# Two quads of saved block products in chunks 2 to 7 of gate and up, and Silu on ScalarE

## The chip, the cores and the metric

The kernel runs on one core of a Trainium2 chip. The metric is the device time of one execution in microseconds (us), the median of three runs. Inside the core, TensorE (PE) multiplies, ScalarE (ACT) and VectorE (DVE) work element by element, GpSimd (POOL) does little here, and SyncE (SP) issues the weight loads. Each engine takes its own instructions strictly in the order written, and waits at semaphores for the others.

## The reference, cut to what matters

The block is a feed-forward net (FFN), a token mixer, and a second FFN, on 256 tokens of width 2048, in float32. Both FFNs have 5632 hidden columns:

```python
def swiglu(x, w_gate, w_up, w_down):
    return (jax.nn.silu(x @ w_gate) * (x @ w_up)) @ w_down

h = layer_norm(ALPHA * h + 0.5 * swiglu(h, w_gate, w_up, w_down), g, b)   # twice, with the mixer between
```

The change concerns the two products `x @ w_gate` and `x @ w_up` of both FFNs and the silu and the product that follow.

## The kernel before, in words

**Units and splits.** The hidden columns are worked in 11 chunks of 512. For a chunk, the 2048 inner rows come as 8 units of 256 rows for the gate and 8 for the up weights. The loads (512 KB each) go to a ring of 8 raw slots, strictly in order; a raw slot is loaded again when VectorE is through with it (`lo_done`). Each float32 number is split in a high part, a copy on ScalarE in a reduced format (`chunk_hi`, L1142), and a low part, a subtraction on VectorE (`chunk_lo`, L1149). The pair lies in one of 4 split slots, which comes free when TensorE has used the item in it (`unit_used`). TensorE waits for the low part and then makes three products a tile, high by high, high by low, low by high (`token_mm`, L628 to L630). A unit is 2 token halves by 2 inner tiles by 3 products, 12 matmuls of 128x128 by 512 columns.

**Quads.** In chunks 2 to 10, one pair (a, b) of the inner units, 6 and 7, is treated together with the gate and the up columns as a 2 by 2 block matrix, for which two token halves would need 8 block products. Winograd's form of Strassen's scheme does it in 7, called P1 to P7, each on one 512-column item with 2 x 3 = 6 matmuls (`chunk_form`, L1266 to L1268). A quad thus takes 7 x 6 = 42 matmuls in place of the 48 of its four units. The price is on the other engines: seven splits in place of four, and four sums of weight blocks on VectorE (`chunk_add`, L1538; they feed the splits of P5, P6, P7 and P4), two seeds of the up accumulators (`up_seeds`, L1546 and L1549) and three ScalarE copies of half accumulators (L1382, L1393, L1398).

P1, P5, P6 and P7 of the next chunk's quad stand in the second half of a chunk, between the up units; P2, P3 and P4 in the first half, between the gate units. A loop chunk of before is this list of 19 items (g gate unit, u up unit):

```
g0 P2 g1 P3 g2 P4 g3 g4 g5 | u0 u1 P1 u2 P5 P6 u3 P7 u4 u5
```

**Order on the engines.** All orders are written out by hand. ScalarE and VectorE run 3 items ahead (`CHUNK_LEAD`), one split an item, the sums and the other work set between splits at fixed items. When the gate is done, ScalarE takes `tanh(0.5 g)` of both halves (`tanh_gate`, L1350), and VectorE makes `(tanh + 1) g` of it in two instructions (`gate_part`, L1490). At the start of a chunk VectorE multiplies the last chunk's gate by its up (`gate_times_up`, L1211, two instructions), then writes the seeds. After item 4 TensorE transposes the 4 x 2 tiles of the last chunk's result (`hT_pe`, L1192), split again by ScalarE and VectorE behind their item 8.

Chunk 0 (16 units) and chunk 1 are written out, chunks 2 to 9 are a hardware loop, chunk 10 is written out.

Of the kernel before, what the change touches and what calls it, by code (L numbers as in the profile page):

```python
# [12 lines left out]
ALU = mybir.AluOpType  # L13
# [6 lines left out]
P = 128  # L20
# [37 lines left out]
class Chunk:  # L58


    def __init__(self, items, raws, slots):
        self.items, self.raws, self.slots = items, raws, slots
# [5 lines left out]
    def raw(self, u, c, ahead):  # L68

        return self.raws.index((u, c, ahead)) if (u, c, ahead) in self.raws else None  # L70

    def used_before(self, i):

        n = len(self.items)
        back = [v for v in range(i) if self.slots[v] == self.slots[i]]
        return back[-1] if back else max(v for v in range(n) if self.slots[v] == self.slots[i]) - n


def chunk_plans(a, b, units):


    def plain(c, us):
        return [("unit", u, c) for u in us]

    some = [u for u in range(units) if u not in (a, b)]
    gate, up = plain(0, some), plain(1, some)
    here = [gate[0], ("P2", 0, 0), gate[1], ("P3", 0, 0), gate[2], ("P4", 0, 0), *gate[3:]]
    ahead = up[:2]
    ahead += [("P1", 0, 0), up[2], ("P5", 0, 0), ("P6", 0, 0), up[3], ("P7", 0, 0), *up[4:]]
    raws_here = [(some[0], 0, 0), (b, 0, 0)] + [(u, 0, 0) for u in some[1:]]  # L90
    u1 = [(u, 1, 0) for u in some]
    raws_ahead = u1[:2] + [(a, 0, 1), (a, 1, 1), u1[2], (b, 1, 1), *u1[3:]]
    lead = plain(0, range(units)) + plain(1, (a, b)) + ahead
    raws_lead = [(u, 0, 0) for u in range(units)] + [(a, 1, 0), (b, 1, 0)] + raws_ahead
    body, last = here + ahead, here + up
    shift = len(here) - 1
    return (Chunk(lead, raws_lead, [i % 4 for i in range(len(lead))]),
            Chunk(body, raws_here + raws_ahead, [(i + (i >= shift)) % 4 for i in range(len(body))]),
            Chunk(last, raws_here + u1, [i % SPLIT_SLOTS for i in range(len(last))]))
# [159 lines left out]
def hybrid_block(nc, x, x_t, ffn1_w_gate, ffn1_w_up, ffn1_w_down, ln1_g, ln1_b, w_in, q_norm_g, kv_norm_g,  # L259
# [40 lines left out]
    (F1GU, F1G1, F1GL, F1GE, F1DA, F1DB, WA, WZ, WB, WC, WQI, WUQ, WO,  # L300
     F2GU, F2G1, F2GL, F2GE, F2DA, F2DB) = range(19)
    QUAD_A, QUAD_B = KU - 2, KU - 1
    CHUNKS = chunk_plans(QUAD_A, QUAD_B, KU)
    LOOP_FROM, LOOP_TO = 2, GATE_CHUNKS - 1
    CHUNK_LEAD = 3

    def gate_up_phases(ffn):

        lead, body, last = CHUNKS
        n, m = len(lead.raws), len(body.raws)  # L310
        assert m % RAW_SLOTS == 0 and (2 * KU) % RAW_SLOTS == 0 and (n + len(last.raws)) % RAW_SLOTS == 0
# [36 lines left out]
    with ExitStack() as ctx:  # L348
# [168 lines left out]
        def split_place(p, it, u):  # L517

            n = st.phases[p].units
            if chunk_of(p) is not None:  # L520
                round, v = divmod(u, n)
                plan, s = chunk_of(p), chunk_of(p).slots[v]
                before = plan.used_before(v)
                if before < 0 and p in (F1G1, F2G1):
                    last = [w for w in range(2 * KU) if ring_place(w, 2 * KU, SPLIT_SLOTS) == s]
                    before = last[-1] - 2 * KU if last else None
                elif before < 0 and p in (F1GE, F2GE):
                    before = CHUNKS[1].used_before(CHUNKS[1].slots.index(s))
                free = None if before is None else st.index(p, it, round * n + before + 1)
                return (whi, wlo, s, free) if s < SPLIT_SLOTS else (chunk_hi4, chunk_lo4, 0, free)  # L530
# [3 lines left out]
            if plan_of(p) is not None:  # L534
                f, pair = (0, 1)[p in DOWN[1]], (0, 1)[p in (F1DB, F2DB)]
                s, before = SPLITS[pair][u] if u < n else (u - n, LAST_USER[u - n])
                if before is not None:
                    free = st.index(DOWN[f][before[0]], 0, before[1] + 1)
                elif s < SPLIT_SLOTS:
                    last = [v for v, slot in enumerate(CHUNKS[2].slots) if slot == s][-1]  # L540
                    free = st.index(GE[f], 0, last + 1)
                else:
                    free = None
# [409 lines left out]
        G1, GL, GE = [F1G1, F2G1], [F1GL, F2GL], [F1GE, F2GE]  # L953
        EXITS, ENTRIES = (F1DB, WO, F2DB), (WA, F2GU)
# [35 lines left out]
        def ffn_loads(sp, f, w_gate, w_up, w_down, load_x):  # L990
# [4 lines left out]
            def released(plan, r):  # L995

                u, c, ahead = plan.raws[r]
                if u == QUAD_B and c == 0 and not ahead and ("P4", 0, 0) in plan.items:
                    return plan.at("P4") - 1
                if (u, c, ahead) == (QUAD_A, 0, 1):  # L1000
                    return plan.at("P1") + 1
                if (u, c, ahead) == (QUAD_A, 1, 1):
                    return plan.at("P7")
                if (u, c, ahead) == (QUAD_B, 1, 1):
                    return len(plan.items) + CHUNKS[1].at("P3")
                return plan.at("unit", u, c)

            def raw_free(p, it, r):

                plan = chunk_of(p)  # L1010
                if r >= RAW_SLOTS:
                    return st.index(p, it, released(plan, r - RAW_SLOTS) + 1)
                if p == G1[f]:
                    return st.index(GU[f], 0, 2 * KU - RAW_SLOTS + r + 1)
                body = CHUNKS[1]
                return st.index(p, it, released(body, len(body.raws) - RAW_SLOTS + r) - len(body.items) + 1)

            lead, body = CHUNKS[:2]
            assert all(released(lead, len(lead.raws) - RAW_SLOTS + r) - len(lead.items)
                       == released(body, len(body.raws) - RAW_SLOTS + r) - len(body.items) for r in range(RAW_SLOTS))  # L1020
# [18 lines left out]
            gate_up(GE[f], 0, GATE_CHUNKS - 1)  # L1039
# [21 lines left out]
        DOWN_SCALE = 0.25 / ALPHA  # L1061
# [11 lines left out]
        BODY_STEPS = ["U4", "V", "P4", "P5", "P6", "P7"]  # L1073
        LOOPS = LOOP_TO - LOOP_FROM
        GU_STEPS = len(SUM_STEPS) + len(BODY_STEPS) * (LOOPS + 1) - 3 + 3
        F_STEPS = GU_STEPS + len(SUM_STEPS) + sum(PAIR_STEPS)
        BODY_ACTS = ["P1 out", "U2 out", "U3 out"]
        GU_ACTS = 4 + len(BODY_ACTS) * (LOOPS + 1)
        F_ACTS = GU_ACTS + 4 + len(PAIRS)

# [4 lines left out]
        def round_of(p, it):  # L1085

            return -1 if p in G1 else LOOPS if p in GE else it

        def in_chunk(f, p, it, step):

            first = F_STEPS * f + len(SUM_STEPS) + len(BODY_STEPS) - 3
            return round_of(p, it) * len(BODY_STEPS) + (first + BODY_STEPS.index(step) + 1)

        def before_chunk(f, p, it, step):

            first = F_STEPS * f + len(SUM_STEPS) - 3
# [2103 lines left out]
```

## Time and profile before

| | |
|---|---|
| median of three runs | 1897.35 us (1897.04 to 1897.39) |
| the profiled execution's own time | 1897.86 us |
| its span, first to last instruction | 1896.1 us |
| PE busy | 1878.8 us, 99% |
| DVE busy | 1428.4 us, 75% |
| ACT busy | 980.6 us, 52% |
| DMA | 189 GB/s mean |
| granted TensorE clock, mean | 0.998 |

The page's busy share of PE counts any matmul in flight, so 99% says that PE hardly ever stood empty. The share of the other engines is a mean over stretches in which they run against a full queue and stretches in which they wait.

### The profile page before, as it was taken

Reading aid. Unit: us, or ns where it says so; the run is one execution under the profiler, and the core shown is the slowest. Engines: PE = TensorE matmul, PEld = TensorE weight load, DVE = VectorE, ACT = ScalarE, POOL = GpSimd, SP = SyncE. Lnnn points to the kernel's source line nnn. Section 1 sums busy time; section 2 is a strip of 40 time slices with the busy share of each in tenths; the row PEclk is TensorE's granted clock in tenths of the full one; section 3 lists DMA queues with packets and bytes.
Section 4 is the critical chain, followed back from the end, with each engine's and each line's share of the span. In section 5 each row is a group of like instructions: output and inputs, shape, how many; then the busy total and the mean of one; then the engine's idle time right before and its main releaser. Section 6 shows DMA issues by size and latency. Waiting matters only on the chain.

```text
span 1896.1 us, 28377 instructions
## 1 busy us (share of the span) xinstructions
PE 1878.8 (99%) x10382; PEld 1602.2 (85%) x10382; DVE 1428.4 (75%) x1601; ACT 980.6 (52%) x1112; POOL 66.9 (4%) x93
## 2 busy tenths in 40 slices
PE   9999999999999999999999999999999999999997
PEld 8888888888888888999999888888888888888886
DVE  5777777777788896677766967677777777688887
ACT  5555555555455553545744534455555555455452
POOL 0000000000000001300131100000000000000000
PEclk9999999999999999999999999999999999999999
DMA  8555566656655584755442067546665555646654
GB/s 304 168 183 177 190 211 213 211 203 217 206 177 189 204 312 118 222 181 150 130 135 91 23 205 261 178 129 213 212 211 188 188 178 198 222 134 222 216 184 188
DMA packets 185375, 357.50 MB, mean 189 GB/s; under 512 B 11328, under 2 KB 23616, under 8 KB 184272
## 3 DMA queue, kind: packets, MB, share of 16 engines
q1 hardware_dynamic: 183600, 347.43, 54.6%
q0 software_dynamic: 1696, 8.99, 1.4%
q8 instruction: 53, 0.87, 0.2%
q14 instruction: 26, 0.21, 0.0%
HBM read 354.28 MB, written 2.10 MB: 188 GB/s over the span
## 4 chain that ended last, share of the span: by engine, by line
PE 95%; DVE 3%; issue 1%; ACT 1%; DMA 0%; POOLq 0%; POOL 0%; DVEq 0%; ACTq 0%
PE acc L628 22%; PE acc L630 21%; PE acc L629 21%; PE acc L652 3%; PE acc L656 3%; PE acc L654 3%; PE acc L1268 3%; PE acc L1266 3%; PE acc L1267 3%; PE tp L1310 1%; PE tp L1312 1%; PE tp L1311 1%; PE tp L1192 1%; PE acc L1310 1%; PE acc L1312 1%; PE acc L1311 1%
## 5 line engine op out<-in xcount | busy, mean ns | idle before, releaser
L1149 DVE TENSOR_TENSOR wlo<-raw,whi 128x1024 fp32r<-128x1024 f32 x248 | 303.3, 1223 | 173.5 <-ACT whi L1142 168.4
L628 PE MATMUL acc<-whi,xT 128*128 128x512 f32 (+2 forms) x1132 | 429.9, 380 | 0.8 <-ACT zab L2095 0.4
L630 PE MATMUL acc<-whi,xT 128*128 128x512 f32 (+2 forms) x1132 | 426.1, 376 | 0.0
L629 PE MATMUL acc<-wlo,xT 128*128 128x512 f32 (+2 forms) x1132 | 425.8, 376 | 0.0
L1142 ACT ACTIVATE whi<-raw 128x1024 fp32r<-128x1024 f32 x248 | 262.9, 1060 | 257.3 <-PE acc L630 159.3
L616 DVE TENSOR_TENSOR wlo<-raw,whi 128x1024 fp32r<-128x1024 f32 (+2 forms) x239 | 277.6, 1169 | 154.3 <-ACT whi L600 152.5
L600 ACT ACTIVATE whi<-raw 128x1024 fp32r<-128x1024 f32 (+2 forms) x239 | 238.0, 1005 | 227.6 <-PE acc L630 159.9
L628 PEld LDWEIGHTS acc<-whi,xT 128*128 128x128 f32 x1132 | 212.6, 188 | 42.4 <-issue 1.7
L630 PEld LDWEIGHTS acc<-whi,xT 128*128 128x128 f32 x1132 | 212.5, 188 | 39.0
L629 PEld LDWEIGHTS acc<-wlo,xT 128*128 128x128 f32 x1132 | 212.7, 188 | 37.8
L628 PE MATMUL acc<-whi,hT 128*128 128x512 f32 x352 | 137.3, 390 | 0.8 <-DVE wlo L616 0.8
L630 PE MATMUL acc<-whi,hT 128*128 128x512 f32 x352 | 137.0, 389 | 0.0
L629 PE MATMUL acc<-wlo,hT 128*128 128x512 f32 x352 | 136.9, 389 | 0.0
L1149 DVE TENSOR_TENSOR chunk_lo<-raw,chunk_hi 128x1024 fp32r<-128x1024 f32 x72 | 88.0, 1223 | 40.1 <-ACT chunk_hi L1142 38.7
L652 PE MATMUL acc<-xT,whi 128*128 128x256 f32 x384 | 108.7, 283 | 0.0
L654 PE MATMUL acc<-xT,whi 128*128 128x256 f32 x384 | 108.7, 283 | 0.0
L656 PE MATMUL acc<-xT,wlo 128*128 128x256 f32 x384 | 108.7, 283 | 0.0
L1142 ACT ACTIVATE chunk_hi<-raw 128x1024 fp32r<-128x1024 f32 x72 | 76.2, 1058 | 60.5 <-PE acc L630 55.7
L630 PE MATMUL acc<-chunk_hi,xT 128*128 128x512 f32 x224 | 87.1, 389 | 0.0
L628 PE MATMUL acc<-chunk_hi,xT 128*128 128x512 f32 x224 | 87.1, 389 | 0.0
L629 PE MATMUL acc<-chunk_lo,xT 128*128 128x512 f32 x224 | 87.1, 389 | 0.0
L1419 ACT ACTIVATE whi<-raw 128x1024 fp32r<-128x1024 f32 x54 | 57.4, 1063 | 45.8 <-PE acc L630 16.0
(432 smaller groups left out, 3376.7 us busy)
## 6 DMA issues: line engine op xcount, KB each, us to landing
raw<-in_ffn_w_down_dram SPq DMA_DIRECT2D x176, 512.0 KB, 6.9
raw<-in_ffn_w_up_dram SPq DMA_DIRECT2D x175, 512.0 KB, 8.1
raw<-in_ffn_w_gate_dram SPq DMA_DIRECT2D x174, 512.0 KB, 4.4
raw<-in_w_in_dram SPq DMA_DIRECT2D x48, 512.0 KB, 3.9
raw<-in_w_out_dram SPq DMA_DIRECT2D x32, 512.0 KB, 6.5
raw<-in_w_in_dram SPq DMA_DIRECT2D x32, 260.0 KB, 2.8
raw<-in_w_in_dram SPq DMA_DIRECT2D x16, 456.0 KB, 7.1
raw<-in_w_q_idx_dram SPq DMA_DIRECT2D x8, 512.0 KB, 3.9
```

The lines of the kernel that those rows point to most:

```text
L600: act.activation(hi[:, s, :, 0:w], raw[:, r, :, 0:w], ACT.Copy).then_inc(hi_done, 1)
L616: dve.tensor_tensor(lo[:, s, :, 0:w], raw[:, r, :, 0:w], hi[:, s, :, 0:w].bitcast(F32), ALU.subtract).then_inc(lo_done, 1)
L628: pe.matmul(o, hi, w_hi[:, s, k, 0:width], start=first and k == 0, stop=False, skip_group_check=seeded)
L629: pe.matmul(o, hi, w_lo[:, s, k, 0:width], start=False, stop=False, skip_group_check=seeded)
L630: ins = pe.matmul(o, lo, w_hi[:, s, k, 0:width], start=False, stop=last and k == UNIT_KT - 1, skip_group_check=seeded)
L652: pe.matmul(o, whi[:, s, k, cols], hi, start=first and k == 0 and c == 0, stop=False, skip_group_check=True)
L654: pe.matmul(o, whi[:, s, k, cols], lo, start=False, stop=False, skip_group_check=True)
L656: ins = pe.matmul(o, wlo[:, s, k, cols], hi, start=False, stop=end, skip_group_check=True)
L1142: act.activation(hi[:, s], src, ACT.Copy).then_inc(hi_done, 1)
L1149: dve.tensor_tensor(lo[:, s], src, hi[:, s].bitcast(F32), ALU.subtract).then_inc(lo_done, 1)
L1266: pe.matmul(o, x_hi, w_hi[:, s, k], start=k == 0 and alone, stop=False, skip_group_check=not alone)
L1419: act.activation(w_hi[:, s], form_raw(p, i), ACT.Copy).then_inc(hi_done, 1)
```

## The change: what it does

- Chunks 2 to 7 get two quads, of inner units (4, 6) and (5, 7); chunks 8 to 10 keep one, (4, 6). Chunks 7, 8 and 9 are now written out (`SINGLE`), the loop holds chunks 2 to 6.
- A loop chunk is now this list of 22 items (P1.0 is of the first quad, P1.1 of the second):

```
P3.0 P3.1 P2.0 g0 P2.1 g1 g2 P4.0 g3 P4.1 | u0 u1 P1.0 P1.1 P5.0 u2 P6.0 P6.1 P5.1 u3 P7.0 P7.1
```

- Products of one kind of both quads add up in the same accumulator, so the copies and seeds stay as many as they were.
- VectorE's sums are now T1 (for P5), T2 (P6), T3 (P7), T4 (P4), one each for every quad, behind the split of a named item. `gate_times_up` ("times") and the first seed ("U4") of the next chunk move to the end of the chunk, behind the splits of its items 22 and 23, that is of the next chunk's items 0 and 1; P3.0 waits for U4. The second seed ("V") stands behind the split of item 3. Before, these three stood at the start of a chunk, whose first item was a gate unit.
- `tanh_gate` and `gate_part` become `silu_gate`: two ScalarE instructions, one a half, and none on VectorE. `DOWN_SCALE` doubles for it.
- In chunk 1 the eight sums of x blocks for the products' other operand are twice as wide, and their splits are made for two quads.
- Slots: item i of a loop chunk lies in split slot (i + [i >= 5] + [i >= 10]) mod 4; of chunk 1 in i mod 4. A raw slot is released by the later of its split's item and its sum's.

```diff
+        (_, b), (_, b2) = quads
+        return ([("P3", 0, 0), ("P3", 1, 0), ("P2", 0, 0), g[0], ("P2", 1, 0), g[1], g[2], ("P4", 0, 0), g[3],
+                 ("P4", 1, 0)],
+                [raws[0], (b, 0, 0), (b2, 0, 0), *raws[1:]], [],
+                {3: [("V", 0, 0)], 4: [("T4", 0, 0)], 5: [("T4", 1, 0)]})
...
+        a2, b2 = quads[1]
+        assert len(u) == 4
+        return ([u[0], u[1], ("P1", 0, 0), ("P1", 1, 0), ("P5", 0, 0), u[2], ("P6", 0, 0), ("P6", 1, 0),
+                 ("P5", 1, 0), u[3], ("P7", 0, 0), ("P7", 1, 0)],
+                [ur[0], ur[1], (a, 0, 1), (a2, 0, 1), (a, 1, 1), ur[2], (b, 1, 1), (a2, 1, 1), (b2, 1, 1), ur[3]],
+                {base + 2: [("T1", 0, 1)], base + 4: [("T2", 0, 1), ("T1", 1, 1)], base + 5: [("T2", 1, 1)],
+                 base + 7: [("T3", 0, 1)], base + 8: [("T3", 1, 1)],
+                 base + 12: [("times", 0, 1)], base + 13: [("U4", 0, 1)]})
...
+    first = make(0, 2, (), 0)
+    first = make(0, 2, (), slots - len(first.items) % slots)
+    body = make(2, 2, (5, 10), 0)
+    assert (len(body.items) + 2) % slots == 0
+    to_one = make(2, 1, (), 0)
+    one = make(1, 1, (), len(to_one.items))
+    one_more = make(1, 1, (), len(to_one.items) + len(one.items))
+    return first, body, to_one, one, one_more, make(1, 0, (), 0, last_slots)
...
-    LOOP_FROM, LOOP_TO = 2, GATE_CHUNKS - 1
+    GATE_QUADS = [(4, 6), (5, 7)]
+    CHUNKS = chunk_plans(GATE_QUADS, KU, SPLIT_SLOTS + 1, SPLIT_SLOTS)
+    LOOP_FROM, LOOP_TO = 2, 7
...
-                if name == "P3":
-                    pe.wait_ge(sem("formed"), in_chunk(f, p, it, "U4"))
...
+                if name == "P3" and q == 0:
+                    pe.wait_ge(sem("formed"), formed_at(p, it, "U4"))
...
-            def tanh_gate(c, used):
+            def silu_gate(c, used):
...
-                act.activation(gated[:], acc0[:], ACT.Tanh, scale=0.5).then_inc(sem("tanh_gate"), 1)
+                for t in range(T):
+                    act.activation(gated[:, t], acc0[:, t], ACT.Silu).then_inc(acc0_free[t], 1)
...
-            def gate_part(c):
-
-                dve.wait_ge(sem("tanh_gate"), c + (f * GATE_CHUNKS + 1))
-                for t in range(T):
-                    dve.scalar_tensor_tensor(out=gated[:, t], in0=gated[:, t], scalar=1.0, in1=acc0[:, t],
-                                             op0=ALU.add, op1=ALU.mult).then_inc(acc0_free[t], 1)
...
+            def up_seed(p, it, c, of):
+
+                dve.wait_ge(unit_used, last_done(p, it, "P5", of))
+                dve.wait_ge(sem("sum_act"), copied(p, it, "U2 out", of))
+                dve.wait_ge(acc1_free[0], c + (n1[GU[f]] + of))
+                dve.tensor_tensor(acc1[:, 0], tp[:, 3], gate_sum[0][:, 1], ALU.add).then_inc(sem("formed"), 1)
...
                 for i in range(CHUNK_LEAD, n + (LEAD if p == GE[f] else CHUNK_LEAD)):
                     split_lo(dve, p, it, i)
...
-                    if i + 2 < n and plan.items[i + 2][0] in ("P4", "P5", "P6", "P7"):
-                        chunk_add(p, it, plan.items[i + 2][0])
-                    if i == gate_end + 3:
-                        gate_part(c)
+                    for what, q, of in plan.after.get(i, ()):
+                        event(p, it, c, what, q, of)
```

## Rows read from the trace of the kernel before

**Rows 1.** The page: span, busy time of each engine, and the chain by engine

```profile
span 1896.1 us, 28377 instructions
...
PE 1878.8 (99%) x10382; PEld 1602.2 (85%) x10382; DVE 1428.4 (75%) x1601; ACT 980.6 (52%) x1112; POOL 66.9 (4%) x93
...
PE 95%; DVE 3%; issue 1%; ACT 1%; DMA 0%; POOLq 0%; POOL 0%; DVEq 0%; ACTq 0%
```

**Rows 2.** Busy time by stage: us, busy us (instructions) of PE, PEld, DVE, ACT, POOL, granted clock, DMA share, GB/s

```profile
197.75:240.81 43.06, 43.06 (x196) 35.74 (x195) 32.01 (x31) 23.36 (x24) 0.00 (x0) 1.00 0.57 193
```

**Rows 3.** Waits, PE alone: for whom, total us, times, longest us

```profile
PE acc L628 <- DVE wlo L616: 0.8, 2, 0.4
```

**Rows 4.** Timeline of PE, end of chunk 5, start of 6: start, us, engine, line, operation

```profile
270.12 0.39 PE L628 MATMUL acc<-chunk_hi,xT 128*128 128x512 f32 x1
...
272.84 0.39 PE L628 MATMUL acc<-whi,xT 128*128 128x512 f32 x1
...
275.56 0.39 PE L1266 MATMUL acc<-whi,xT 128*128 128x512 f32 x1
...
276.92 0.39 PE L628 MATMUL acc<-whi,xT 128*128 128x512 f32 x1
```

**Rows 5.** The chain in order of time, eight transposes of chunk 5: start, us

```profile
240.81 0.87 PE tp L1192 x8
```

**Rows 6.** Timeline of ACT, DVE and SPq, chunks 5 and 6: [idle before <-releaser]

```profile
263.52 0.60 ACT L1382 ACTIVATE gate_sum<-acc 128x512 f32<-128x512 f32 x1 [0.30 <-PE acc L1268]
...
264.01 1.05 ACT L1142 ACTIVATE chunk_hi<-raw 128x1024 fp32r<-128x1024 f32 x1
...
273.04 1.06 ACT L1142 ACTIVATE chunk_hi<-raw 128x1024 fp32r<-128x1024 f32 x1 [1.66 <-PE acc L630]
273.04 1.28 DVE L1211 TENSOR_TENSOR gated<-gated,acc 128x512 f32<-128x512 f32 x2 [0.40 <-PE acc L630]
...
274.24 0.69 DVE L1546 TENSOR_TENSOR acc<-tp,gate_sum 128x512 f32<-128x512 f32 x1
...
274.84 0.69 DVE L1549 TENSOR_TENSOR acc<-tp,gate_sum 128x512 f32<-128x512 f32 x1
...
275.44 1.21 DVE L1149 TENSOR_TENSOR chunk_lo<-raw,chunk_hi 128x1024 fp32r<-128x1024 f32 x1
...
276.57 1.22 DVE L1538 TENSOR_TENSOR gate_sum<-raw,gate_sum 128x1024 f32<-128x1024 f32 x1
...
276.82 1.61 SPq L1027 DMA_DIRECT2D raw<-in_ffn_w_gate_dram  x3
...
277.71 1.22 DVE L1149 TENSOR_TENSOR wlo<-raw,whi 128x1024 fp32r<-128x1024 f32 x1
...
277.90 1.06 ACT L1142 ACTIVATE whi<-gate_sum 128x1024 fp32r<-128x1024 f32 x1 [1.07 <-DVE gate_sum L1538]
...
279.00 1.23 DVE L1149 TENSOR_TENSOR wlo<-gate_sum,whi 128x1024 fp32r<-128x1024 f32 x1
...
280.75 1.06 ACT L1142 ACTIVATE whi<-raw 128x1024 fp32r<-128x1024 f32 x1 [1.79 <-DMA raw<-in_ffn_w_gate_dram]
```

**Rows 7.** Timeline near 36 us: a VectorE split and the matmuls that wait for it

```profile
35.61 1.23 DVE L616 TENSOR_TENSOR wlo<-raw,whi 128x1024 fp32r<-128x1024 f32 x1 [3.17 <-ACT whi L600]
...
36.98 0.47 PE L628 MATMUL acc<-whi,xT 128*128 128x512 f32 x1
...
37.29 0.40 PE L629 MATMUL acc<-wlo,xT 128*128 128x512 f32 x1
```

**Rows 8.** Groups of ScalarE instructions: count | busy us, mean ns | idle us before

```profile
L1350 ACT ACTIVATE gated<-acc 128x1024 f32<-128x1024 f32 x22 | 22.6, 1027 | 16.2 <-PE acc L630 16.2
...
L600 ACT ACT_TABLE_LOAD x5 | 6.4, 1283 | 0.1
```

More of the change, by code:

```diff
@@ L58, with __init__ @@
 class Chunk:
-    def __init__(self, items, raws, slots):
-        self.items, self.raws, self.slots = items, raws, slots
+    def __init__(self, items, raws, skips, first_slot, slots, start, after, quads_here, quads_ahead):
+        self.items, self.raws = items, raws
+        self.slots = [(first_slot + i + sum(i >= k for k in skips)) % slots for i in range(len(items))]
+        self.start, self.after = start, after
+        self.quads_here, self.quads_ahead = quads_here, quads_ahead
     def at(self, what, x=0, c=0):
@@ L66, in at @@
         return self.items.index((what, x, c))
[L68 to L99, printed above, removed]
@@ new lines, in last, with gate_end, events, chunk_plans @@
+    def last(self, kind):
+        return max(i for i, item in enumerate(self.items) if item[0] == "unit" and item[2] == kind)
+    def gate_end(self):
+        own = ("P2", "P4") if self.quads_here else ()
+        return max(i for i, item in enumerate(self.items)
+                   if item[0] in own or (item[0] == "unit" and item[2] == 0))
+    def events(self):
+        return [*self.start, *(e for i in sorted(self.after) for e in self.after[i])]
+def chunk_plans(quads, units, slots, last_slots):
+    def plain(c, n):
+        return [("unit", u, c) for u in range(units) if all(u not in q for q in quads[:n])]
+    def here(n):
+        if n == 0:
+            return plain(0, 0), [(u, 0, 0) for u in range(units)], [("times", 0, 0)], {}
+        g = plain(0, n)
+        raws = [(u, 0, 0) for _, u, _ in g]
+        if n == 1:
+            (_, b), = quads[:1]
+            return ([g[0], ("P2", 0, 0), g[1], ("P3", 0, 0), g[2], ("P4", 0, 0), *g[3:]],
+                    [raws[0], (b, 0, 0), *raws[1:]], [("times", 0, 0), ("U4", 0, 0), ("V", 0, 0)], {3: [("T4", 0, 0)]})
+        (_, b), (_, b2) = quads
[3 more added lines that the diff above has]
+                {3: [("V", 0, 0)], 4: [("T4", 0, 0)], 5: [("T4", 1, 0)]})
+    def ahead(n, ups, base):
+        u, ur = ups, [(u, 1, 0) for _, u, _ in ups]
+        if n == 0:
+            return u, ur, {}
+        a, b = quads[0]
+        if n == 1:
+            return ([u[0], u[1], ("P1", 0, 0), u[2], ("P5", 0, 0), ("P6", 0, 0), u[3], ("P7", 0, 0), *u[4:]],
+                    [ur[0], ur[1], (a, 0, 1), (a, 1, 1), ur[2], (b, 1, 1), *ur[3:]],
+                    {base + 2: [("T1", 0, 1)], base + 3: [("T2", 0, 1)], base + 5: [("T3", 0, 1)]})
+        a2, b2 = quads[1]
[6 more added lines that the diff above has]
+                 base + 12: [("times", 0, 1)], base + 13: [("U4", 0, 1)]})
+    def make(n_here, n_ahead, skips, first_slot, n_slots=slots):
+        items, raws, start, after = here(n_here)
+        if n_here:
+            ups = plain(1, n_here)
+        else:
+            ups = plain(1, n_ahead)
+            more = [item for item in plain(1, 0) if item not in ups]
+            items, raws = items + more, raws + [(u, 1, 0) for _, u, _ in more]
+        more, more_raws, later = ahead(n_ahead, ups, len(items))
+        return Chunk(items + more, raws + more_raws, skips, first_slot, n_slots, start, {**after, **later},
+                     n_here, n_ahead)
+    first = make(0, 2, (), 0)
[6 more added lines that the diff above has]
+    return first, body, to_one, one, one_more, make(1, 0, (), 0, last_slots)
@@ L521, in split_place @@
                 round, v = divmod(u, n)
[L522 to L528, printed above, removed]
+                s, before = chunk_of(p).slots[v], slot_used_before(p, v)
                 free = None if before is None else st.index(p, it, round * n + before + 1)
@@ L539, in split_place @@
                 elif s < SPLIT_SLOTS:
-                    last = [v for v, slot in enumerate(CHUNKS[2].slots) if slot == s][-1]
+                    last = [v for v, slot in enumerate(CHUNKS[-1].slots) if slot == s][-1]
                     free = st.index(GE[f], 0, last + 1)
@@ L993, in ffn_loads, with raw_free, before @@
             down_v = w_down.rearrange("(k p) n -> p k n", p=P)
[L995 to L1020, printed above, removed]
+            def raw_free(p, r):
+                def before(c):
+                    g = RAWS_AT[c] + r - RAW_SLOTS
+                    item = g if g < 2 * KU else raw_released(g)
+                    return item - CHUNK_AT[c] + 1
+                return same([before(c) for c in chunks_of(p)])
             def gate_up(p, it, c):
@@ new lines, in hybrid_block @@
+        for c, plan in enumerate(PLAN_OF):
+            if plan is None:
+                continue
+            for what, q, of in plan.events():
+                if what != "times":
+                    steps += 1
+                    FORMED[c + of, what, q] = steps
+            for i, (what, q, _) in enumerate(plan.items):
+                if what != "unit":
+                    FORM_AT[c + (what in ("P1", "P5", "P6", "P7")), what, q] = CHUNK_AT[c] + i
+            for i, events in plan.after.items():
+                for what, q, of in events:
+                    MADE_AT[c + of, what, q] = CHUNK_AT[c] + i + 1
+            if plan.quads_ahead:
+                for name in COPIES:
+                    copies += 1
+                    COPIED[c + 1, name] = copies
@@ L1076, in hybrid_block, with raw_released @@
+        GU_STEPS, GU_ACTS = steps, copies
         F_STEPS = GU_STEPS + len(SUM_STEPS) + sum(PAIR_STEPS)
-        BODY_ACTS = ["P1 out", "U2 out", "U3 out"]
-        GU_ACTS = 4 + len(BODY_ACTS) * (LOOPS + 1)
         F_ACTS = GU_ACTS + 4 + len(PAIRS)
+        LOOP_STEPS = sum(e[0] != "times" for e in CHUNKS[1].events())
+        SUM_OF = {"P5": "T1", "P6": "T2", "P7": "T3", "P4": "T4"}
+        def raw_released(g):
+            c = max(c for c in range(1, GATE_CHUNKS) if RAWS_AT[c] <= g)
+            plan = PLAN_OF[c]
+            u, kind, ahead = plan.raws[g - RAWS_AT[c]]
+            if ahead == 0 and ("unit", u, kind) in plan.items:
+                return CHUNK_AT[c] + plan.at("unit", u, kind)
+            a, b = zip(*GATE_QUADS)
+            if ahead == 0:
+                q = b.index(u)
+                return max(FORM_AT[c, "P2", q], MADE_AT[c, "T4", q])
+            if u in b:
+                q = b.index(u)
+                return max(FORM_AT[c + 1, "P3", q], MADE_AT[c + 1, "T3", q])
+            q = a.index(u)
+            return max(FORM_AT[c + 1, "P1", q], MADE_AT[c + 1, "T1", q]) if kind == 0 else FORM_AT[c + 1, "P7", q]
@@ new lines, in event @@
+            def event(p, it, c, what, q, of):
+                if what == "times" and of:
+                    gate_times_up(dve, f, c + 1, st.index(p, it, chunk_of(p).last(1) + 1))
+                elif what == "times":
+                    gate_times_up(dve, f, c, st.index(p, it, 0))
+                elif what == "U4":
+                    up_seed(p, it, c, of)
+                elif what == "V":
+                    second_up_seed(p, it, c)
+                else:
+                    chunk_sum(p, it, what, q)
@@ L1602, in chunk @@
                 n = len(plan.items)
-                gate_end = plan.at("unit", QUAD_B if p == G1[f] else KU - 3, 0)
-                gate_times_up(dve, f, c, st.index(p, it, 0))
-                if p != G1[f]:
-                    up_seeds(p, it, c)
+                for what, q, of in plan.start:
+                    event(p, it, c, what, q, of)
                 for i in range(CHUNK_LEAD, n + (LEAD if p == GE[f] else CHUNK_LEAD)):
```

322 lines of the change are left out of this document (181 added, 141 removed).

## The prediction

> **What bounds the kernel now.** I read the page first: PE is busy for 99% of the span and 95% of the chain that ended last is PE [rows 1]. The reader is to see that nothing else sets the end. Then the stages: a loop chunk takes 43.06 us, all of it PE at the full granted clock (2.4 GHz), with VectorE at 32.01 us and ScalarE at 23.36 [rows 2]. The waits of PE name weight splits for 0.8 us in the whole execution, and none of them is a split of chunks 1 to 10, which are line L1149 [rows 3]. So a chunk costs what its matmuls cost, and a matmul less is time gained as long as the splits keep up.
>
> **What a chunk costs.** From the first matmul of a unit to the next unit's, 270.12 to 272.84, is 2.72 us for 12 matmuls; a block product, 275.56 to 276.92, is 1.36 for 6 [rows 4]; the transposes add 0.87 [rows 5]. The old list has 12 units and 7 products: 32.64 + 9.52 + 0.87 = 43.03, the measured period [rows 2]. The new one has 8 units and 14 products: 21.76 + 19.04 + 0.87 = 41.67. Each second quad saves 1.36 us; six chunks in two FFNs have one, so PE's own work shrinks by 12 x 1.36 = 16.3 us.
>
> **What the other engines get.** VectorE's splits and sums start 1.13 and 1.14 us apart when nothing holds them (275.44, 276.57, 277.71); I take 1.135. A 512-wide instruction takes 0.60 (274.24, 274.84), the two of `gate_times_up` 1.20 (273.04 to 274.24) [rows 6]. Per loop chunk VectorE gains three splits and four sums, 7 x 1.135 = 7.95 us, and loses `gate_part`, two instructions, about 1.2: 32.0 becomes some 38.7 of busy time in 41.7 us. That fits as a mean. The question is the second half, where the eight products stand.
>
> **Handoffs**, each read off the rows. PE done to the ScalarE or VectorE instruction that waits for it: 272.84 to 273.04, 0.20. ScalarE split to VectorE split: 277.90 to 279.00, 1.09 to 1.10. Sum on VectorE to the ScalarE split of it: 276.57 to 277.90, 1.33 [rows 6]. VectorE split to the matmul that waits: the second matmul of the run starts at 37.29, so the first really ran 0.227 before, at 37.06, 1.45 after 35.61 [rows 7]. A 512-wide seed is 0.69 long instead of 1.23 [rows 6, 7], so 0.91 to the matmul.
>
> **Timetable of the new second half.** Zero is when PE ends item 9 (P4.1). With four slots, item 12 (P1.0) takes the slot of item 9, so its ScalarE split starts at 0.20, its VectorE split at 1.29. This start cannot be earlier. From there VectorE goes without pause, but for two gaps of 0.15 (P5.0's split waits for T1.0, P6.1's for T2.1, each 1.33 + 1.09 after the sum, one split lying between):
>
> - split 12 at 1.29, T1.0 2.43, split 13 3.56, split 14 (P5.0) 4.85, T2.0 5.98, T1.1 7.12, split 15 (u2) 8.25. PE: u0 and u1 to 5.44, three products to 9.52; u2 may start at 8.25 + 1.45 = 9.70: a wait of 0.18.
> - T2.1 9.39, split 16 10.52, split 17 (P6.1) 11.81, T3.0 12.94, split 18 (P5.1) 14.08, ready 15.53. PE: u2 to 12.42, P6.0 and P6.1 to 15.14: wait 0.39.
> - T3.1 15.21, split 19 (u3) 16.35, ready 17.80; PE ends P5.1 at 16.89: wait 0.91. u3 ends at 20.52.
> - splits 20, 21 and 22 at 17.48, 18.62 and 19.75; `times` needs u3 (20.72) and VectorE (20.89), so 20.89; split 23 at 22.09 (ScalarE's half, behind u3, is there at 21.81), U4 at 23.22, and P3.0 of the next chunk at 24.13. PE ended P7.1 at 20.52 + 2.72 = 23.24: wait 0.89.
>
> Sum: 24.13 us against 4 x 2.72 + 8 x 1.36 = 21.76 of matmuls, 2.37 us of waits. One line checks it: 0.20 + 1.09 to the first split, 18 instructions of 1.135 (20.43), two gaps (0.30), `times` 1.20, U4 0.91. Behind the waiting matmul stands all of PE's work, so the waits go straight into the time.
>
> In the first half VectorE has 10 splits, T4.0, T4.1, V and one part of the transposed result, 13 x 1.135 + 0.60 = 15.4 us, beside 19.91 us of PE (4 units, 6 products, transposes); in the same kind of timetable each split there is ready over 1.3 us before PE comes to it. The waits are not made up, for four slots allow no longer lead. The period becomes 24.13 + 19.91 = 44.04, against 43.06: 1.0 us longer. The same timetable on the old list has no wait, a period of 43.04, and puts T4 3.73 us behind the chunk's start; the rows have 276.57 - 272.84 = 3.73 [rows 4, 6].
>
> **Chunk 1** keeps slots i mod 4, so P1.0's split can start one unit earlier. Zero now at u1's end: split 17 1.97, T2.1 3.11, split 18 4.24, split 19 5.53, T3.0 6.66, split 20 7.80, T3.1 8.93, split 21 (u3) 10.07, ready 11.52 against PE's 10.88: 0.64 of wait, then the 0.89 at P3.0 as before. The wider x sums stand beside its gate units, which leave VectorE 1.6 us free each. Chunk 7 has two quads in its first half and one in its second, chunks 8 to 10 the old pattern: no waits.
>
> **Edits at nothing.** Silu is two ScalarE instructions of 0.49 to 0.5 each (263.52 to 264.01 is such a copy) for one of 1.03 [rows 6, 8], done by 2.2 in the timetable, before P1.0 at 5.44. Without that cover it would cost at most its second 0.5. The same 16 loads go out per chunk. The tightest is P2.1's: its slot is released by split 20, the issue comes 1.38 later (275.44 to 276.82), the data 3.93 after (to 280.75) [rows 6], at 22.8; its split cannot start before P3.0 is done, 25.7: 2.9 us in hand. Peeling chunks 7 to 9 changes no order.
>
> **The sum.** Per FFN: five loop chunks x 2.37 + (0.64 + 0.89) = 13.4 us of waits, less 6 x 1.36 = 8.2: +5.2. Two FFNs: +10.4. The profiled execution is 1897.86 us (its span 1896.1 and 1.8 around it), 0.5 over the median of 1897.35; so the new median is 1897.35 + 10.4 = 1907.8.
>
> **A rule on ScalarE's tables.** The only table loads among the groups are in the mixer and at the start, 1283 ns each, the five of L600 with 0.1 us of idle before them together [rows 8]; chunks 1 to 10 have none between Tanh and copies. The Trainium skill, "ScalarE: Activation LUTs", Table sets: the hidden batching unit, says that cheap functions such as copy lie in every set. By it Silu and the copies share a set, and a load or two at the FFNs' borders is all. Its section What ACT_TABLE_LOAD costs adds a drain of about 1.38 us, which the 0.1 us here does not show. If copies did force a switch, that is rival C.
>
> **Rivals.**
> - A, PE stays the bound: no waits, 1897.35 - 16.3 = 1881.1. For it: no split is waited for now, and the mean load fits. Against: the chain above would have to shrink to 21.76, an instruction every 1.00 us on VectorE where the rows have 1.135. Point of decision against before: 24.13 less 1.0, a spacing of 1.08.
> - B, only the wait for U4 bites, because the second half's splits somehow have more lead: -16.3 + 12 x 0.89 = -5.6, 1891.7. For it: chunk 1's slots show what one item more of lead is worth. Against: slot of item 12 is that of item 9, by the code.
> - C, slower still by ScalarE: a table load of 1.28 behind Silu in each quad chunk. Split 13 then starts at 4.53 instead of 3.56, all behind it 0.97 later: 12 x 0.97 = +11.6, 1919.4. Against: rows 8.
> - D, the terms cancel: waits of some 1.36 a chunk (say a spacing of 1.08), within 0.2%. Nothing in the rows speaks for it.
>
> **The numbers.** Forecast 0.78, A 0.08, B 0.05, C 0.05, D 0.04. Under the forecast, a spacing of 1.13 or 1.14 moves the sum by 12 x 18 x 0.005 = 1.1, uncertain handoffs (0.1 in the chain per chunk) by 1.2, and I allow 3 for delays that no row shows, such as the longer lists of semaphores: its own range is 1905 to 1912. The range reaches further to both sides, 1899 to 1914. A measurement tells 0.2% (3.8 us). Faster by more: A and B, 0.13. Within: D, 0.04. Slower: 0.83.
>
> **What would show it.** Right: transposes 44.0 us apart in the loop; PE idle four times a loop chunk, three behind VectorE splits of u2, P5.1 and u3 and one, 0.9 us, behind the seed at P3.0; VectorE without a gap over 0.2 us from P1.0's split to U4; ScalarE waiting for VectorE's sums. Wrong: a period of 41.7, or PE waiting for ScalarE or a load, or table loads in the chunks.

## The result, and the profile after

| | before | after |
|---|---|---|
| median of five runs | 1897.35 us | 1907.61 us (1906.99 to 1907.87) |
| ratio, 95% interval | 1 | 1.0053 (1.0040 to 1.0067) |
| profiled execution, span | 1896.1 us | 1905.9 us |
| matmuls (PE instructions) | 10382 | 10310 |

The kernel became slower by 10.3 us, against 10.4 forecast (1907.8). The 72 matmuls that were to go are gone (12 quads x 6).

The page after (span, busy time by engine, chain by engine), beside [rows 1]:

```profile
span 1905.9 us, 27915 instructions
...
PE 1873.3 (98%) x10310; PEld 1585.8 (83%) x10310; DVE 1498.8 (79%) x1649; ACT 1024.7 (54%) x1181; POOL 66.9 (4%) x93
...
PE 79%; DVE 13%; issue 5%; ACT 2%; DMA 1%; DVEq 0%; POOL 0%; POOLq 0%; ACTq 0%
```

PE's share of the chain that ended last fell from 95% to 79%, and VectorE's rose from 3% to 13%: the end of the kernel is now set on two engines. PE's busy share tells little of it, 98% for 99%.

One loop chunk of after, from transposes to transposes, in the columns of [rows 2]:

```profile
248.13:292.22 44.09, 42.76 (x190) 34.33 (x189) 38.48 (x36) 26.38 (x28) 0.00 (x0) 1.00 0.58 190
```

It takes 44.09 us for 43.06, with PE busy 42.76 and VectorE 38.48 (32.01 before), which is 87% of it.

PE's waits that name VectorE (total us, times, longest us); before there was no row for lines of chunks 1 to 10:

```profile
PE acc L1361 <- DVE acc L1654: 8.1, 12, 0.7
PE acc L704 <- DVE wlo L1245: 6.8, 12, 0.6
```

L1361 is the first matmul of a block product, and the seed L1654 (U4) releases it, 12 times: the 12 chunk borders at which P3.0 comes first. L704 is a unit's first matmul, 12 times behind a split. The page counts less than PE lost, since a matmul in flight counts as busy for 0.39 us though the next could start 0.227 after it: a lost 0.88 (at u3, below) shows as 0.62, and the losses at u2 and P5.1, 0.13 and 0.30, have no row at all.

VectorE in one second half, start us and duration; the reader is to lay it beside the timetable of the prediction, whose zero is here 259.77:

```profile
262.20 1.22 DVE L1633 TENSOR_TENSOR gate_sum<-raw 128x1024 f32<-128x1024 f32 x1
263.33 1.22 DVE L1245 TENSOR_TENSOR chunk_lo<-raw,chunk_hi 128x1024 fp32r<-128x1024 f32 x1
264.62 1.23 DVE L1245 TENSOR_TENSOR wlo<-gate_sum,whi 128x1024 fp32r<-128x1024 f32 x1
265.77 1.22 DVE L1637 TENSOR_TENSOR gate_sum<-raw,gate_sum 128x1024 f32<-128x1024 f32 x1
266.90 1.22 DVE L1633 TENSOR_TENSOR gate_sum<-raw 128x1024 f32<-128x1024 f32 x1
268.04 1.22 DVE L1245 TENSOR_TENSOR wlo<-raw,whi 128x1024 fp32r<-128x1024 f32 x1
269.17 1.22 DVE L1637 TENSOR_TENSOR gate_sum<-raw,gate_sum 128x1024 f32<-128x1024 f32 x1
270.31 1.22 DVE L1245 TENSOR_TENSOR wlo<-gate_sum,whi 128x1024 fp32r<-128x1024 f32 x1
271.52 1.22 DVE L1245 TENSOR_TENSOR chunk_lo<-gate_sum,chunk_hi 128x1024 fp32r<-128x1024 f32 x1
272.67 1.22 DVE L1641 TENSOR_TENSOR raw<-raw 128x1024 f32<-128x1024 f32 x1
273.80 1.22 DVE L1245 TENSOR_TENSOR wlo<-gate_sum,whi 128x1024 fp32r<-128x1024 f32 x1
274.94 1.22 DVE L1641 TENSOR_TENSOR raw<-raw 128x1024 f32<-128x1024 f32 x1
276.07 2.35 DVE L1245 TENSOR_TENSOR wlo<-raw,whi 128x1024 fp32r<-128x1024 f32 x2
278.34 1.22 DVE L1245 TENSOR_TENSOR chunk_lo<-raw,chunk_hi 128x1024 fp32r<-128x1024 f32 x1
279.48 1.22 DVE L1245 TENSOR_TENSOR wlo<-raw,whi 128x1024 fp32r<-128x1024 f32 x1
280.61 1.28 DVE L1307 TENSOR_TENSOR gated<-gated,acc 128x512 f32<-128x512 f32 x2
281.81 1.22 DVE L1245 TENSOR_TENSOR wlo<-raw,whi 128x1024 fp32r<-128x1024 f32 x1
282.94 0.69 DVE L1654 TENSOR_TENSOR acc<-tp,gate_sum 128x512 f32<-128x512 f32 x1
```

From T1.0 (262.20) to the split of u3 (276.07, the first of the two there) and on to the seed U4 (282.94) VectorE never pauses for more than the 0.15 us ahead of P5.0's split (264.62) over its spacing of 1.13 to 1.15. The timetable has T1.0 at 2.43, split 15 at 8.25, split 19 at 16.35 and U4 at 23.22, that is 262.20, 268.02, 276.12 and 282.99.

PE at u2, P5.1, u3 and P3.0 in the same stretch (start us, length; the next matmul shows when the first really ran):

```profile
269.31 0.50 PE L704 MATMUL acc<-whi,xT 128*128 128x512 f32 x1
269.64 0.39 PE L705 MATMUL acc<-wlo,xT 128*128 128x512 f32 x1
...
275.07 0.50 PE L1361 MATMUL tp<-whi,sumX 128*128 128x512 f32 x1
275.41 0.40 PE L1363 MATMUL tp<-wlo,sumX 128*128 128x512 f32 x1
```

```profile
277.34 0.50 PE L704 MATMUL acc<-whi,xT 128*128 128x512 f32 x1 [0.62 <-DVE wlo L1245]
...
277.68 0.39 PE L705 MATMUL acc<-wlo,xT 128*128 128x512 f32 x1
```

```profile
283.77 0.49 PE L1361 MATMUL acc<-whi,sumX 128*128 128x512 f32 x1 [0.69 <-DVE acc L1654]
...
284.10 0.40 PE L1363 MATMUL acc<-wlo,sumX 128*128 128x512 f32 x1
```

277.68 less 0.227 is 277.45, 1.38 us after the split of u3 began; the longer lengths, 0.50 and 0.49 for 0.39, are another sign of a matmul that waited. P3.0 ran at 284.10 - 0.23 = 283.87; the timetable's 24.13 is 283.90. In the same way u2 ran at 269.41 and P5.1 at 275.18. Against 0.227 behind the matmul before each (those started at 269.06, 274.66, 276.34 and 282.69), PE lost 0.13 us at u2, 0.30 at P5.1, 0.88 at u3 and 0.95 at P3.0; the forecast has 0.18, 0.39, 0.91 and 0.89.

### The profile page after: what moved, and what is told of

Its sections match the earlier page's. It is cut to its first block, busy times and chain, and to the rows that moved or that the text cites. A ratio compares the mean times of both kernels' runs of the same rounds, so it can differ in the third digit from the quotient of the medians.

```text
span 1905.9 us, 27915 instructions
## 1 busy us (share of the span) xinstructions
PE 1873.3 (98%) x10310; PEld 1585.8 (83%) x10310; DVE 1498.8 (79%) x1649; ACT 1024.7 (54%) x1181; POOL 66.9 (4%) x93
## 3 DMA queue, kind: packets, MB, share of 16 engines
q8 instruction: 62, 1.02, 0.2%
## 4 chain that ended last, share of the span: by engine, by line
PE 79%; DVE 13%; issue 5%; ACT 2%; DMA 1%; DVEq 0%; POOL 0%; POOLq 0%; ACTq 0%
PE acc L704 16%; PE acc L706 16%; PE acc L705 16%; DVE wlo L1245 4%; PE acc L728 3%; PE acc L732 3%; PE acc L730 3%; PE acc L1361 3%; PE acc L1364 3%; PE acc L1363 3%; DVE gate_sum L1633 1%; DVE gate_sum L1637 1%; ACT whi L1238 1%; PE tp L1407 1%; PE tp L1408 1%
## 5 line engine op out<-in xcount | busy, mean ns | idle before, releaser
L692 DVE TENSOR_TENSOR wlo<-raw,whi 128x1024 fp32r<-128x1024 f32 (+2 forms) x239 | 277.6, 1170 | 158.8 <-ACT whi L676 156.9
L1238 ACT ACTIVATE whi<-raw 128x1024 fp32r<-128x1024 f32 x252 | 267.1, 1060 | 240.9 <-PE acc L706 163.2
L704 PE MATMUL acc<-whi,xT 128*128 128x512 f32 (+2 forms) x996 | 380.9, 382 | 7.9 <-DVE wlo L1245 6.8
L706 PE MATMUL acc<-whi,xT 128*128 128x512 f32 (+2 forms) x996 | 373.9, 375 | 0.0
L705 PE MATMUL acc<-wlo,xT 128*128 128x512 f32 (+2 forms) x996 | 373.5, 375 | 0.0
L704 PEld LDWEIGHTS acc<-whi,xT 128*128 128x128 f32 x996 | 187.2, 188 | 51.2 <-DVE wlo L1245 14.8
L706 PEld LDWEIGHTS acc<-whi,xT 128*128 128x128 f32 x996 | 187.2, 188 | 33.6
L705 PEld LDWEIGHTS acc<-wlo,xT 128*128 128x128 f32 x996 | 187.4, 188 | 31.4
L704 PE MATMUL acc<-whi,hT 128*128 128x512 f32 x352 | 137.6, 391 | 1.1 <-DVE wlo L692 1.1
L1245 DVE TENSOR_TENSOR chunk_lo<-raw,chunk_hi 128x1024 fp32r<-128x1024 f32 x68 | 83.2, 1223 | 19.4 <-ACT chunk_hi L1238 18.0
L1238 ACT ACTIVATE whi<-gate_sum 128x1024 fp32r<-128x1024 f32 x68 | 72.0, 1058 | 41.0 <-PE acc L706 23.3
L1245 DVE TENSOR_TENSOR wlo<-gate_sum,whi 128x1024 fp32r<-128x1024 f32 x68 | 83.1, 1223 | 11.9 <-ACT whi L1238 8.6
L1238 ACT ACTIVATE chunk_hi<-raw 128x1024 fp32r<-128x1024 f32 x68 | 71.9, 1058 | 38.1 <-PE acc L706 27.8
L1536 ACT ACTIVATE whi<-raw 128x1024 fp32r<-128x1024 f32 x54 | 57.4, 1062 | 43.9 <-PE acc L706 16.1
L704 PEld LDWEIGHTS acc<-whi,hT 128*128 128x128 f32 x352 | 66.1, 188 | 15.8 <-issue 1.6
```

The costliest lines, as they stand in the source:

```text
L692: dve.tensor_tensor(lo[:, s, :, 0:w], raw[:, r, :, 0:w], hi[:, s, :, 0:w].bitcast(F32), ALU.subtract).then_inc(lo_done, 1)
L704: pe.matmul(o, hi, w_hi[:, s, k, 0:width], start=first and k == 0, stop=False, skip_group_check=seeded)
L705: pe.matmul(o, hi, w_lo[:, s, k, 0:width], start=False, stop=False, skip_group_check=seeded)
L706: ins = pe.matmul(o, lo, w_hi[:, s, k, 0:width], start=False, stop=last and k == UNIT_KT - 1, skip_group_check=seeded)
L1238: act.activation(hi[:, s], src, ACT.Copy).then_inc(hi_done, 1)
L1245: dve.tensor_tensor(lo[:, s], src, hi[:, s].bitcast(F32), ALU.subtract).then_inc(lo_done, 1)
```

## The experiments

All times are medians; "before" ran on the same chip for each group at 1897.24 us (e1 to e4) and 1897.42 us (e5 to e8).

| run | what differs | expected us | measured us | ratio to before, 95% | loop period us |
|---|---|---|---|---|---|
| after | | 1907.8 | 1907.61 | 1.0053 (1.0040 to 1.0067) | 44.06 |
| e1 | seed U4 earlier | 1896.9 | 1895.78 | 0.9994 (0.9985 to 1.0003) | 43.10 |
| e2 | sums T1 earlier | 1891.1 | 1891.31 | 0.9967 (0.9955 to 0.9980) | 42.55 |
| e3 | both | 1881.0 | 1881.00 | 0.9914 (0.9900 to 0.9927) | 41.71 |
| e4 | before with Silu alone | 1897.3 | 1898.25 | 1.0004 (0.9995 to 1.0013) | 43.07 |
| e5 | slots skip at 5 and 6 | 1899.4 | 1899.11 | 1.0011 (1.0001 to 1.0020) | 43.20 |
| e6 | after without T3 | 1891.4 | 1893.30 | 0.9979 (0.9969 to 0.9988) | 42.73 |
| e7 | after with Tanh | 1919.5 | 1917.66 | 1.0109 (1.0092 to 1.0126) | 45.08 |
| e8 | e3 with Tanh | 1892.5 | 1891.33 | 0.9965 (0.9951 to 0.9980) | 42.77 |

The periods are the distance of the transposes between about 200 and 340 us, over three chunks. The theory: PE waits because what VectorE does from P1.0's split to the seed, 18 splits and sums and the two instructions of `times`, takes in its written order longer than the matmuls beside it. The rivals: four slots cannot feed three products in a row whatever VectorE does; VectorE's total load is the bound, not its order; Silu costs.

**e1, the seed earlier.**

```diff
-                 base + 12: [("times", 0, 1)], base + 13: [("U4", 0, 1)]})
+                 base + 12: [("times", 0, 1), ("U4", 0, 1)]})
```

> One edit to the kernel after: the first seed of the up accumulators (U4) stands right behind the product gate x up, ahead of the split of item 23, in chunks 1 to 6. Theory (waits come from VectorE's order in the second half): PE waits 0.89 us less at P3.0 at each of 12 chunk borders, loop period 43.15 us in place of 44.04, total 10.7 us less than after: 1896.9 us; the 1.47 us of waits at u2, P5.1 and u3 stay. Rival (slots: three products in a row outrun four split slots whatever VectorE does; the wait at P3.0 is only where PE's surplus lead ends up): taking it away there moves it to the next split, period stays 44.0, 1907.6 us.

Measured: 1895.78 us. PE's waits for VectorE in chunks 1 to 10:

```profile
PE acc L704 <- DVE wlo L1245: 6.7, 12, 0.6
```

The row of the seed is gone, and that of the splits is what it was, 6.7 us in 12 (6.8 after). Swapping two VectorE instructions brought back 11.8 us, 1.1 more than expected; the wait taken away was 0.95 long and not 0.89, which is 0.7 of it. The wait did not move to the next split, so the rival of the slots fails here.

**e2, the sums T1 where VectorE stood idle.**

```diff
-                {base + 2: [("T1", 0, 1)], base + 4: [("T2", 0, 1), ("T1", 1, 1)], base + 5: [("T2", 1, 1)],
+                {base: [("T1", 0, 1)], base + 1: [("T1", 1, 1)], base + 4: [("T2", 0, 1)], base + 5: [("T2", 1, 1)],
```

> One edit to the kernel after: the sums T1 of both quads stand behind the splits of u0 and u1 (where VectorE waits for ScalarE) in place of behind P1.0's and P5.0's; same work in all. Theory: VectorE's chain from P1.0's split on is two instructions shorter and both gaps behind it go; the three waits in the second half vanish, only the one at P3.0 stays (0.86 us), total 16.5 us less than after: 1891.1 us, loop period 42.5 us. Rival (slots): the waits at u2, P5.1 and u3 stay, since the items and slots are unchanged: 1907.6 us. Rival (VectorE's total load is the bound, not its order): no change either.

Measured: 1891.31 us, 16.3 less than after.

```profile
PE acc L1361 <- DVE acc L1654: 6.7, 12, 0.6
```

Now the row of the splits is gone and the seed's alone is left. Neither the work of any engine, nor the items, nor their split slots were changed, so both rivals in their plain form, slots whatever VectorE does and total load, are out. Where VectorE stood idle is seen in after, ahead of its split at 256.98, and in e2 the sum has taken a part of that time:

```profile
256.98 1.23 DVE L1245 TENSOR_TENSOR wlo<-raw,whi 128x1024 fp32r<-128x1024 f32 x1 [2.85 <-ACT whi L1238]
259.70 2.59 DVE L1245 TENSOR_TENSOR wlo<-raw,whi 128x1024 fp32r<-128x1024 f32 x2 [1.50 <-ACT whi L1238]
```

```profile
253.02 1.22 DVE L1633 TENSOR_TENSOR gate_sum<-raw 128x1024 f32<-128x1024 f32 x1
254.60 1.23 DVE L1245 TENSOR_TENSOR wlo<-raw,whi 128x1024 fp32r<-128x1024 f32 x1 [0.36 <-ACT whi L1238]
```

**e3, both edits.**

> Both edits together (seed behind the product gate x up, sums T1 behind the splits of u0 and u1). Theory: no wait of PE is left in chunks 1 to 7, period 41.68 us, all of the 16.3 us of saved matmuls is seen: 1881.0 us, 26.7 less than after. Rival (VectorE at some 90% in a loop chunk cannot keep up whatever the order): at best 1890 to 1900 us.

Measured: 1881.00 us, 26.6 less than after and 16.2 less than before. A loop chunk, and the first row of PE's waits that names a VectorE split:

```profile
239.64:281.36 41.72, 41.72 (x190) 34.61 (x189) 38.13 (x36) 26.13 (x28) 0.00 (x0) 1.00 0.60 201
```

```profile
PE acc L704 <- DVE wlo L692: 1.2, 3, 0.4
```

PE is busy for all of 41.72 us, within 0.05 of the matmuls' own 41.67, beside a VectorE that is busy 38.13 us of it, 91%. The waits left are none of a split of chunks 1 to 10 (L692 is the split of the other stages). This is the version that beats both kernels.

**e4, Silu alone.** The kernel before with this edit (its main lines), `gate_part` removed and the down scale doubled:

```diff
-                act.activation(gated[:], acc0[:], ACT.Tanh, scale=0.5).then_inc(sem("tanh_gate"), 1)
+                for t in range(T):
+                    act.activation(gated[:, t], acc0[:, t], ACT.Silu).then_inc(acc0_free[t], 1)
```

> The kernel before with Silu on ScalarE alone (two instructions of 512 in place of one Tanh of 1024, no second step on VectorE, the down scale doubled). Theory: nothing waits for either there, 1897.3 us, within 0.1%; two more table loads of 1.28 us, hidden. Rival (Silu costs: a table switch in each chunk, or on PE's path at the entry of an FFN): 2 to 28 us more.

Measured: 1898.25 us; the interval takes in no change, and the period is that of before. In the groups of ScalarE:

```profile
L1351 ACT ACTIVATE gated<-acc 128x512 f32<-128x512 f32 x44 | 23.9, 595 | 14.9 <-PE acc L630 14.9
...
L1351 ACT ACT_TABLE_LOAD x2 | 2.6, 1283 | 0.0
...
L2350 ACT ACT_TABLE_LOAD x1 | 1.3, 1283 | 0.0
```

Three table loads more than before: one for the first Silu of each FFN, and a third ahead of the first Exp in the mixer (L2350), which the kernel before doesn't have. There is none in the chunks between Silu and copies. Not all of them are hidden. The first FFN's load stands in chunk 0, and PE waits behind it:

```profile
35.16 1.28 ACT L1351 ACT_TABLE_LOAD   x1
...
39.90 0.47 PE L628 MATMUL acc<-whi,xT 128*128 128x512 f32 x1 [0.38 <-DVE wlo L616]
```

The matmul before that one started at 39.13 and the one behind it at 40.20, so PE lost 0.61 us there. The same wait is in the traces of after, e3 and e6, which all have Silu, and not in those of before, e7 and e8, which have Tanh. That is 0.6 of the 1.0 us by which the medians differ; the rest can't be told at this precision.

**e5, the slots.**

```diff
-    body = make(2, 2, (5, 10), 0)
+    body = make(2, 2, (5, 6), 0)
```

> One number changed in the kernel after: the split slots of a loop chunk skip at items 5 and 6 in place of 5 and 10, so that P1.0's split takes the slot of item 8, not 9, and can start one product (1.36 us) earlier; VectorE's order is as in after. Theory: the chain starts earlier, u2's and P5.1's waits go, u3's falls to 0.64, P3.0's stays at 0.89: 8.4 us less than after, 1899.4 us, loop period 43.2 us.

Measured: 1899.11 us.

```profile
PE acc L1361 <- DVE acc L1654: 7.8, 12, 0.7
PE acc L704 <- DVE wlo L1245: 3.1, 12, 0.3
```

The seed's row stays (7.8 us for 8.1), the splits' falls from 6.8 to 3.1. PE lost 0.51 us at u3 (0.64 expected), 0.91 at P3.0, and nothing at u2 and P5.1. The slots do matter, but as the start of VectorE's chain: one product earlier gave 8.5 us. After e1 and e2 this is part of the theory, not a rival to it.

**e6, two sums left out.** The events T3 of the double quads are removed (the first of three places), and P7's split waits for its load instead, so P7 is made of the raw block.

```diff
-                 base + 7: [("T3", 0, 1)], base + 8: [("T3", 1, 1)],
```

> The kernel after without the two sums T3 where the next chunk has two quads: P7's items are split straight from the raw block, so the products P7 are of wrong data; matmuls, splits and loads are all there. Theory: VectorE's chain is two instructions (2.27 us) shorter behind P6.1's split; waits at P5.1 and u3 go, 0.18 at u2 and 0.72 at P3.0 stay: 16.2 us less than after, 1891.4 us, period 42.6 us. Rival (run lengths against slots): unchanged 1907.6 us.

Measured: 1893.30 us, 1.9 more than expected.

```profile
PE acc L1360 <- DVE acc L1653: 6.5, 12, 0.6
```

As expected only the seed's row is left. The period is 42.73 for an expected 42.58, which over ten loop chunks is 1.5 of the 1.9 us. The timeline shows most of it: PE lost 0.82 us at P3.0 where 0.72 was expected (and 0.13 at u2 for 0.18), and the period without waits, e3's, is 41.71 and not 41.67.

**e7 and e8, more work in the same place.** Tanh and the two instructions of `gate_part` (1.19 us) put back, behind P1.0's split (and, in after's order, T1.0), in the order of after (e7) and of e3 (e8). The part on VectorE:

```diff
+                    if i == plan.gate_end() + 3:
+                        gate_part(c)
```

> The kernel after with Tanh on ScalarE and the two-instruction second step on VectorE back in their old place (behind the split of P1.0 and T1.0). Theory: 1.19 us more in VectorE's chain, all of it seen as a longer wait at u2 in the five loop chunks of each FFN, none in chunk 1: 11.9 us more than after, 1919.5 us, period 45.2 us. Rival: nothing, as in the kernel before, where VectorE had room for it.

> e3_both with the same Tanh and second step on VectorE back. Theory: the better order has some slack but less than 1.19 us: waits of 1.15 us a loop chunk come back at P5.1 and u3, 11.5 us more than e3_both: 1892.5 us. Rival (with the better order VectorE is no bound any more): 1881 us.

Measured: 1917.66 us, 10.1 more than after, and 1891.33 us, 10.3 more than e3. The transposes of two loop chunks of e7, then PE's waits in e7 and in e8:

```profile
250.47 0.88 PE tp L1288 x8
...
295.60 0.88 PE tp L1288 x8
```

```profile
PE acc L704 <- DVE wlo L1245: 15.7, 22, 0.9
PE acc L1361 <- DVE acc L1662: 8.1, 12, 0.7
```

```profile
PE acc L704 <- DVE wlo L1245: 6.1, 10, 0.6
```

45.13 us from one to the other. In e7 the seed's row is as in after (8.1), and the splits' grew from 6.8 to 15.7 us: what is added to VectorE behind P1.0's split is seen by PE almost in full, 10.1 of 11.9 us (1.19 x 10 loop chunks). The 1.8 us short of it has two parts in the traces. The pause of 0.15 us ahead of P5.0's split takes up a part of the addition: that split starts 1.13 us behind the one before it in e7, for 1.29 in after, and the period grew by 1.02 and not 1.19. And without Silu's table load the wait of 0.61 us in chunk 0 is gone. In e8 ten waits came back, one a loop chunk, and the period grew from 41.71 to 42.77, 1.06 for 1.19: e3's order has a slack of only some 0.13 us there, an estimate from these periods. Both came out below what was expected, by 1.8 and 1.2 us. In the kernel before, taking the same instructions out gained nothing (e4).

## Why the prediction was right, point by point

- **What bounds the kernel, and 16.3 us saved on PE:** right. 72 matmuls fewer, and with the waits away (e3) the kernel is 16.2 us faster than before.
- **VectorE's load, 38.7 us in a chunk:** 38.48 measured.
- **The timetable of the second half, 24.13 us against 21.76:** every VectorE instruction stands within 0.06 us of the trace, and P3.0 within 0.03. Two links were mis-sized by 0.07 us. P6.1's split started 1.21 us behind the split before it (270.31 to 271.52) where I had 1.29: ScalarE began on the sum T2.1 1.26 us after its start (269.17 to 270.43) and not 1.33. And from a chunk's split to the matmul that waits it is 1.38 us (276.07 to 277.45) for the 1.45 that I read off another stage, so u3 ran 0.12 us ahead of the timetable.
- **Period 44.04:** 44.06, from 204.06 to 336.23 in three chunks.
- **Waits of 0.91 at u3 and 0.89 at P3.0:** 0.88 and 0.95 in the timeline, shown by the two rows of PE's waits, each 12 times, and by e1 and e2, which take them away separately. The 0.18 at u2 and the 0.39 at P5.1 are too short for a row of waits; the timeline shows 0.13 and 0.30. The four come to 2.26 us for 2.37.
- **Chunk 1, 0.64 + 0.89:** from transposes to transposes chunk 1 took 54.21 us (61.67 to 115.88) for 49.88 before. The terms give 1.53 of waits and 2.72 of matmuls, 4.25, for the measured 4.33: chunk 1 holds four products more (5.44), and ahead of the next transposes stand four products and a unit where two products and three units stood (2.72 less). Of the waits the timeline shows 0.57 at u3 and 0.96 at P3.0.
- **Sum, +5.2 us an FFN:** the first FFN's last transposes came at 498.99 us for 493.78, 5.21 later; the second's gate and up took 437.29 us for 432.22, 5.07. The stages between and behind them differ by +0.5 and -1.0 us, which I had at nothing. The first is within what the stage varies by from trace to trace (737.97 to 739.05 us in the ten kernels). The second is not: it took 232.1 and 232.8 us in before and e4, and 230.9 to 231.4 in all eight kernels with the new lists; the cause stays open. So it is partly luck that the sum came within 0.2 us: +0.6 of Silu's table load, -1.0 and the start-up, none of which the prediction had, nearly cancel, and single executions of one kernel differ by more (1896.3 to 1899.3 us for before).
- **Silu at nothing:** right in the loop and for the verdict (e4), but not quite nothing. Its two instructions are 0.59 us long each and hold ScalarE for 0.95 together (260.93 to 261.88):

```profile
L1448 ACT ACTIVATE gated<-acc 128x512 f32<-128x512 f32 x44 | 23.7, 590 | 10.4 <-PE acc L706 9.9 <-PE acc L1364 0.5
...
L1448 ACT ACT_TABLE_LOAD x2 | 2.6, 1283 | 0.0
```

The two loads of 1.28 us are one an FFN, with 0.0 us of idle before them; the third, in the mixer, I had not counted. The one in chunk 0 of the first FFN sits on PE's path:

```profile
34.91 1.28 ACT L1448 ACT_TABLE_LOAD   x1
...
39.65 0.47 PE L704 MATMUL acc<-whi,xT 128*128 128x512 f32 x1 [0.38 <-DVE wlo L692]
```

PE lost 0.61 us there, as in e4. The prediction gave Silu cover in the loop's second half and did not look at chunk 0. The load of the second FFN costs nothing: Silu waits for PE behind it. The trace agrees with what the Trainium skill says in "ScalarE: Activation LUTs", Table sets: the hidden batching unit, that copies lie in every set: none of the chunks between has a load. It again shows nothing of the drain of about 1.38 us that its section What ACT_TABLE_LOAD costs adds: the copy ahead of the load at 34.91 ends at 34.90, and Silu starts at 36.21, 0.02 us behind the load.

Rivals B and C fail on the rows above: PE's waits for the splits are there, and no chunk of the loop has a table load. Rival A (1881.1) was wrong of this kernel, but only because of the places of three VectorE instructions: e3 is that case, at 1881.00. I had put its point of decision at a spacing of VectorE's instructions that the rows exclude, and did not see that the same chain is also shortened by starting its first sums in VectorE's idle time. That bears on the verdict on the idea, not on the forecast of the kernel.

## What to carry to other kernels

When PE's work is traded for work on the engine that feeds it, a mean load does not settle it (PE waits beside a VectorE busy for 87% of the chunk in after, and does not beside one busy for 91% in e3); write the timetable of the one stretch where the new work stands, from the instruction whose start is fixed by a slot to the one that PE waits for, and compare it with the matmuls beside it. If it is longer, look first for sums whose inputs are ready earlier and which can stand where the feeding engine idles, and for the instruction with a waiting matmul behind it, which belongs ahead of those that nobody waits for yet. Here three instructions moved were worth 26.6 us, more than the 16.3 that the whole change was about.

## What the runs showed of the hardware that was not expected

A row of PE's waits shows about 0.26 us less than PE lost (0.88 as 0.62, 0.95 as 0.69, in e5 0.51 as 0.24), and losses of 0.13 and 0.30 have no row. In after the two rows sum to 14.9 us, where PE lost some 26.6 (16.3 of matmuls saved and 10.3 of time added; e3 is 26.6 faster). In e3, where VectorE is busy for 91% of the chunk beside a DMA at 60%, it kept its spacing of 1.13 to 1.15 us from P1.0's split to `times`, with one of 1.22. A table load of 1.28 us took no more than its own 1.28 us of ScalarE, and cost PE 0.61.
